# MLP in blocks of 1024 columns, two of eight k-tile groups by Strassen's seven products

## The chip, the cores and the metric

The kernel runs on one core of one Trainium2 chip. The metric is device time in microseconds of one execution; lower is better. The profile was taken of one such execution.

## What is computed

One decoder layer for 256 tokens with a model width of 2048, in fp32: three token mixers in parallel (gated convolution, attention with decay, attention to memory), merged by gates and projected, and then an MLP with a hidden width of 8192. Only the MLP is changed:

```python
h2 = _rms(x, norm2_g)
x = x + jnp.square(jax.nn.relu(h2 @ w_up)) @ w_down
```

`w_up` is 2048 x 8192 and `w_down` 8192 x 2048, each 64 MB in fp32.

## The kernel before, in words

Every large product runs in the same way. The stationary operand of TensorE is a 128 x 128 tile of activations (the tokens are two tiles of 128), the moving one is 512 columns of a weight row tile. To keep fp32 accuracy with the fp32r format each operand is split into a high part, its rounding, and a low part, the remainder, and each product is three matmuls: low x high, high x high, high x low (`products`, line 1083, matmuls at line 1096).

Weights come in pieces of 2 k tiles x 512 columns (512 KB) in a ring of four buffers, `raw`, `whi` and `wlo`. A piece passes through four engines: SyncE issues its load once the low part of the piece four earlier has been made (`load`, line 346, issue at line 353); ScalarE rounds it to `whi` once it has landed and TensorE has used the piece four earlier (`split`, lines 467 to 473); VectorE subtracts to get `wlo` (lines 718 to 721); TensorE does 2 k tiles x 2 token tiles x 3 = 12 matmuls on it. ScalarE and VectorE run through one fixed list of steps each, written out piece by piece; all other work is hung on piece numbers in that list.

A block is 8 pieces, 512 output columns for all 256 tokens, in two PSUM banks; blocks alternate between banks 0, 1 and 2, 3, so a block is emptied while the next one is computed. Banks 4 to 7 take transposes. The MLP has four quarters of the hidden width. In each, four up blocks give 2048 hidden columns: ScalarE applies the scale and relu from PSUM to `stage` (`relu`, line 663), VectorE squares (`square`, line 1004), TensorE transposes (line 1113, four 128 x 128 tiles to a bank), and ScalarE and VectorE write the high and low parts to `act_parts` (`plain_hi`, line 653, `plain_lo`, line 759). Four down blocks then multiply by `w_down` and VectorE adds the banks to `x_sb` (`add_to_x`, line 999). The first quarter is written out, the other three are a loop on every engine. At the end the last two bank tiles are added (line 1077) and stored in two transfers (line 438).

## Time and profile before

| | us |
|---|---|
| median of 3 runs | 1656.94 (1656.36 to 1657.6) |
| the profiled execution, its own time | 1656.12 |
| its span, first to last instruction | 1654.4 |
| TensorE busy, 7500 matmuls | 1646.7 |
| weight loads of TensorE busy | 1363.3 |
| VectorE busy | 911.1 |
| ScalarE busy | 750.1 |

PE is TensorE, PEld its weight loads, DVE VectorE, ACT ScalarE, SP SyncE, and SPq its queue of DMA issues. In a line of a timeline the first number is the start in us from the span's start, the second the time taken; "x2" means that two instructions were merged; brackets hold the idle time before it and what ended it. Matmuls are pipelined, so the durations of neighbours overlap.

### The profile page before, as it was taken

How to read it: one execution, taken by the hardware profiler on the slowest of the kernel's cores; microseconds unless marked ns; L12 is line 12 of the kernel's file. 1: busy time of each engine (PE TensorE's matmuls, PEld its weight loads, DVE VectorE, ACT ScalarE, POOL GpSimd, SP SyncE). 2: the span in 40 equal slices, each digit the busy share in tenths (PEclk: the TensorE clock that was granted, in tenths of full speed). 3: DMA queues.
4: the chain of work that ended last, by engine and by line, in shares of the span. 5: the costliest groups of instructions: out<-in, count | busy, mean ns of one | idle time of the engine just before them, and what ended most of it. 6: DMA issues, size and time to landing. Idle time of an engine off the chain costs nothing.

```text
span 1654.4 us, 19971 instructions
## 1 busy us (share of the span) xinstructions
PE 1646.7 (100%) x7500; PEld 1363.3 (82%) x7500; DVE 911.1 (55%) x1004; ACT 750.1 (45%) x878; POOL 4.8 (0%) x13
## 2 busy tenths in 40 slices
PE   9999999999999999999999999999999999999998
PEld 7888888888888888888888888888888888888887
DVE  5856666545565444456665555545555555555553
ACT  6744444443444444444445544434443444334432
POOL 0000000000000000000000000000000000000000
PEclk9999999999999999999999999999999999999999
DMA  9856555566566666665655666666566665666554
GB/s 336 280 167 187 166 168 164 154 179 176 166 184 186 192 195 194 191 193 182 197 186 185 186 185 179 198 192 189 181 191 193 191 187 184 195 192 184 184 189 152
DMA packets 160176, 313.49 MB, mean 189 GB/s; under 512 B 9584, under 2 KB 9968, under 8 KB 159600
## 3 DMA queue, kind: packets, MB, share of 16 engines
q1 hardware_dynamic: 160112, 312.62, 62.2%
q8 instruction: 42, 0.69, 0.2%
q14 instruction: 22, 0.18, 0.0%
HBM read 310.49 MB, written 2.10 MB: 189 GB/s over the span
## 4 chain that ended last, share of the span: by engine, by line
PE 98%; DMA 1%; DVE 0%; ACT 0%; SPq 0%; issue 0%; DVEq 0%; ACTq 0%
PE bank L1096 94%; PE bank L1113 2%; PE bank L1125 1%; DMA raw<-in_w_mem_kv 1%; PE bank L1220 0%; PE bank L1150 0%; PE bank L1181 0%; DVE wlo L721 0%; PE bank L1240 0%; ACT whi L473 0%; PE bank L1145 0%; PE bank L1242 0%; DVE wide L806 0%; SPq L362 0%; PE bank L1151 0%
## 5 line engine op out<-in xcount | busy, mean ns | idle before, releaser
L721 DVE TENSOR_TENSOR wlo<-raw,whi 128x1024 fp32r<-128x1024 f32 x574 | 701.5, 1224 | 673.1 <-ACT whi L473 670.2
L473 ACT ACTIVATE whi<-raw 128x1024 fp32r<-128x1024 f32 x574 | 608.2, 1060 | 778.5 <-PE bank L1096 764.6
L1096 PE MATMUL bank<-whi,lhs_a 128*128 128x512 f32 x1920 | 597.6, 392 | 0.0
L1096 PE MATMUL bank<-whi,lhs_b 128*128 128x512 f32 x1536 | 476.5, 391 | 2.0 <-DVE wlo L744 1.3
L1096 PEld LDWEIGHTS bank<-whi,lhs_a 128*128 128x128 f32 x1920 | 357.1, 188 | 71.8
L1096 PE MATMUL bank<-wlo,lhs_a 128*128 128x512 f32 x960 | 374.3, 390 | 0.0
L1096 PEld LDWEIGHTS bank<-whi,lhs_b 128*128 128x128 f32 x1536 | 285.9, 188 | 61.4 <-issue 3.5
L1096 PE MATMUL bank<-whi,act_parts 128*128 128x512 f32 x1024 | 316.1, 390 | 0.0
L1096 PE MATMUL bank<-wlo,lhs_b 128*128 128x512 f32 x768 | 299.3, 390 | 0.0
L1096 PEld LDWEIGHTS bank<-whi,act_parts 128*128 128x128 f32 x1024 | 191.7, 188 | 39.4
L1096 PEld LDWEIGHTS bank<-wlo,lhs_a 128*128 128x128 f32 x960 | 180.2, 188 | 38.3
L1096 PE MATMUL bank<-wlo,act_parts 128*128 128x512 f32 x512 | 199.3, 389 | 0.0
L1096 PEld LDWEIGHTS bank<-wlo,lhs_b 128*128 128x128 f32 x768 | 144.2, 188 | 30.5
L1096 PEld LDWEIGHTS bank<-wlo,act_parts 128*128 128x128 f32 x512 | 96.1, 188 | 20.1
L482 ACT ACTIVATE wide<-bank,sm 128x512 f32<-128x512 f32 (+1 forms) x48 | 30.4, 684 | 36.8 <-PE bank L1096 36.4
L1096 PE MATMUL bank<-whi,y_parts 128*128 128x512 f32 x128 | 40.1, 394 | 0.0
L1004 DVE TENSOR_TENSOR stage<-stage 128x1024 f32<-128x1024 f32 x16 | 19.6, 1225 | 27.3 <-ACT stage L663 27.3
L663 ACT ACTIVATE stage<-bank,sm 128x512 f32<-128x512 f32 x32 | 20.3, 685 | 26.6 <-PE bank L1096 26.6
L999 DVE TENSOR_TENSOR x_sb<-bank,x_sb 128x512 f32<-128x512 f32 x38 | 24.5, 686 | 8.3 <-PE bank L1096 8.3
L1096 PEld LDWEIGHTS bank<-whi,y_parts 128*128 128x128 f32 x128 | 23.6, 188 | 4.7
L1096 PE MATMUL bank<-wlo,y_parts 128*128 128x512 f32 x64 | 25.0, 391 | 0.0
L1113 PEld LDWEIGHTS bank<-ident,stage 128*128 128x128 f32 x160 | 19.8, 139 | 5.2
(133 smaller groups left out, 472.1 us busy)
## 6 DMA issues: line engine op xcount, KB each, us to landing
raw<-in_w_in SPq DMA_DIRECT2D x208, 512.0 KB, 3.7
raw<-in_w_up SPq DMA_DIRECT2D x128, 512.0 KB, 3.7
raw<-in_w_down SPq DMA_DIRECT2D x128, 512.0 KB, 3.8
raw<-in_w_out SPq DMA_DIRECT2D x32, 512.0 KB, 3.7
raw<-in_w_mem_kv SPq DMA_DIRECT2D x30, 512.0 KB, 6.3
raw<-in_w_conv_out SPq DMA_DIRECT2D x16, 512.0 KB, 3.8
raw<-in_w_fox_out SPq DMA_DIRECT2D x16, 512.0 KB, 3.9
raw<-in_w_mem_out SPq DMA_DIRECT2D x16, 512.0 KB, 4.5
```

What stands on the lines that cost most here:

```text
L473: act.activation(whi[n % RING][:], raw[n % RING][:], ACT.Copy).then_inc(hi_ready, 1)
L482: last = act.activation(outs[tok], src, func, scale=scale[:, tok:tok + 1])
L663: last = act.activation(stage[:, tok, :], bank[2 * (b % 2) + tok][:], ACT.Relu, scale=r_2[:, tok:tok + 1])
L721: dve.tensor_tensor(wlo[n % RING][:], raw[n % RING][:], whi[n % RING][:].bitcast(F32), ALU.subtract).then_inc(lo_ready, 1)
L999: last = dve.tensor_tensor(v, bank[2 * (b % 2) + tok][:], v, ALU.add)
L1004: dve.tensor_tensor(stage[:], stage[:], stage[:], ALU.mult).then_inc(sq_ready, 1)
L1096: last = pe.matmul(dst, lhs[:, part, k + kk, s], w[:, kk, :], start=(k + kk == 0 and i == 0), stop=(k + kk == tiles - 1 and i == 2))
L1113: last = pe.transpose(bank[tr_bank(g)][:, P * i:P * (i + 1)], src, ident[:])
L1125: last = pe.matmul(dst, a, b, start=(i == 0), stop=(i == len(pairs) - 1))
```

## The change

The MLP is computed in 16 blocks of 1024 columns, per quarter two up blocks and two down blocks of 8 groups; a group is 2 k tiles x 1024 columns, two pieces (left and right). In six groups each piece takes 12 matmuls as before, the left one into banks 0 and 1, the right one into banks 2 and 3. In groups 3 and 6 the product of the 2 x 2 tiles of activations (2 token tiles x 2 k tiles) with the 2 x 2 tiles of weights (2 k tiles x 2 halves of 512 columns) is done with Strassen's seven products (Winograd's form), each of three matmuls. Three of them add straight into the banks C12, C21 and C11, and P5, P6, P7 and P1 are summed over both groups in banks 4 to 7.

For this VectorE makes four sums of raw weight tiles, T (`t_sums`), which ScalarE rounds and VectorE subtracts (`sums_hi`, `sums_lo`); only tiles 1 to 3 of such a group are split themselves (`split_fast`, 1536 columns in one instruction for both pieces). Four sums of activation tiles, S, are made once per quarter and group (`a_copy`, `s_sums`, `s_hi`, `s_lo`). At the turn of a block ScalarE copies P1 and then banks 0, 1 and banks 2, 3 to SBUF (`c_copy`, into `stage` and `junk`), VectorE makes the corrections from P5, P6, P7 and the copy of P1 (`combine`), and adds them: for an up block to the copies, with relu and square both on ScalarE after it; for a down block x is first added to the corrections (`x_to_sums`) and later the copies (`result`). The transposes of the activations now use banks 4 to 7 ahead of group 3. `act_parts` shares its space with `lhs_a`, and the last block of `w_out` uses banks 4 and 5.

The core of the diff (the engine programs; the helpers for S, the operand parts and the loads' order are left out):

```diff
+FAST = (3, 6)
+GROUPS = KT // PK
+WIDE = 2 * COLS
+FF_BLOCKS = 2 * D // WIDE
+UPS = D // WIDE
+FF_PIECES = FF_BLOCKS * 2 * GROUPS
+C22, C12, C21, C11, P5, P6, P7, P1 = range(8)
+S_1, S_2, S_3, S_4 = range(4)
+T_3, T_1, T_2, T_4 = range(4)
+def ff_piece(q, blk=0, g=0):
...
+                def c_copy(blk, side):
+                    at = FF_BLOCKS * q + blk
+                    act.wait_ge(piece_used, by_n + (ff_piece(q, blk) - 1 + side))
+                    act.wait_ge(ff_done, by_8 + 2 * (at - 1))
+                    act.wait_ge(tr_made, by_8 + (G_FF + GROUPS * (q if blk else q - 1) + 4 * min((blk - 1) % FF_BLOCKS, UPS)))
+                    act.activation(halves[side], bank_all[:, 2 * side:2 * side + 2, :], ACT.Copy).then_inc(c_out, 1)
...
+                for blk in range(FF_BLOCKS):
+                    after = q > 0 or blk > 0
+                    after_up = 0 < blk <= UPS
+                    at = FF_BLOCKS * q + blk
+                    left(blk, 0)
+                    if after:
+                        act.wait_ge(piece_used, by_n + (ff_piece(q, blk) - 2))
+                        act.wait_ge(ff_done, by_8 + 2 * (at - 1))
+                        act.activation(comb[:, 3, :], bank[P1], ACT.Copy).then_inc(p1_copied, 1)
+                    right(blk, 0)
+                    if after:
+                        c_copy(blk, 0)
+                        c_copy(blk, 1)
+                    left(blk, 1)
+                    right(blk, 1)
+                    if after_up:
+                        relu_square(blk, 0)
+                    left(blk, 2)
+                    if after_up:
+                        relu_square(blk, 1)
+                    right(blk, 2)
+                    sums_hi(2 * at, base=by_8)
+                    if after_up:
+                        act_hi(blk, 0)
+                    fast(blk, 3)
+                    if after_up:
+                        act_hi(blk, 1)
+                    left(blk, 4)
+                    right(blk, 4)
+                    if q == 0 and blk == 0:
+                        s_hi(1, 1, s_up)
+                    if after_up:
+                        s_hi(2 * q + blk + 1, blk - 1, s_down, base=2 * i)
+                    left(blk, 5)
+                    right(blk, 5)
+                    sums_hi(2 * at + 1, base=by_8)
+                    fast(blk, 6)
+                    left(blk, 7)
+                    right(blk, 7)
...
+            def t_sums(n, i, base=0, base16=0):
+                for u in range(2):
+                    dve.wait_ge(landed[(n + u) % RING], base16 + 16 * ((n + u) // RING + 1))
+                r = n % RING
+                b = raw_all[:, r:r + 2, :].rearrange("p r (k n) -> p (r k) n", k=PK)
+                b22, b21 = b[:, 1, :], b[:, 3, :]
+                dve.tensor_tensor(t_raw[:, 0:2, :], b[:, 1:3, :], b[:, 0:1, :].to_broadcast([P, 2, COLS]),
+                                  ALU.subtract).then_inc(t_made, 1)
+                dve.wait_ge(t_made, base * 3 + (3 * i + 1))
+                dve.tensor_tensor(t_raw[:, T_2, :], t_raw[:, T_1, :], b22, ALU.add).then_inc(t_made, 1)
+                dve.wait_ge(t_made, base * 3 + (3 * i + 2))
+                dve.tensor_tensor(t_raw[:, T_4, :], b21, t_raw[:, T_2, :], ALU.subtract).then_inc(t_made, 1)
+            def sums_lo(i, base=0):
+                dve.wait_ge(t_hi_ready, base * 2 + 2 * (i + 1))
+                dve.tensor_tensor(t_lo[:], t_raw[:], t_hi[:].bitcast(F32), ALU.subtract).then_inc(t_lo_ready, 1)
+            def split_fast(n, base=0):
+                r = n % RING
+                dve.wait_ge(hi_ready, base + (n + 2))
+                src, hi, lo = [w[:, r:r + 2, :].rearrange("p r n -> p (r n)")[:, COLS:]
+                               for w in (raw_all, whi_all, wlo_all)]
+                dve.tensor_tensor(lo, src, hi.bitcast(F32), ALU.subtract).then_inc(lo_ready, 2)
+            def combine(at, base=0):
+                dve.wait_ge(p1_copied, base + (at + 1))
+                dve.tensor_tensor(comb[:, 4, :], bank[P6], comb[:, 3, :], ALU.add).then_inc(combined, 1)
+                dve.wait_ge(combined, base * 3 + (3 * at + 1))
+                dve.tensor_tensor(comb[:, 2, :], bank[P7], comb[:, 4, :], ALU.add).then_inc(combined, 1)
+                dve.wait_ge(combined, base * 3 + (3 * at + 2))
+                dve.tensor_tensor(comb[:, 0:2, :], comb[:, 2:5:2, :],
+                                  bank[P5].unsqueeze(1).to_broadcast([P, 2, COLS]),
+                                  ALU.subtract).then_inc(combined, 1)
...
+            def x_to_sums(at, c, base=0):
+                dve.wait_ge(combined, base * 3 + 3 * (at + 1))
+                for side in range(2):
+                    v = comb[:, 2 * side:2 * side + 2, :]
+                    last = dve.tensor_tensor(v, v, x_half(c, side), ALU.add)
+                last.then_inc(x_in, 1)
+            def result(at, side, dst, base=0):
+                dve.wait_ge(c_out, base * 2 + (2 * at + side + 1))
+                dve.tensor_tensor(dst, halves[side], comb[:, 2 * side:2 * side + 2, :],
+                                  ALU.add).then_inc(ff_done, 1)
...
+                for blk in range(FF_BLOCKS):
+                    after = q > 0 or blk > 0
+                    after_up = 0 < blk <= UPS
+                    after_down = after and not after_up
+                    at = FF_BLOCKS * q + blk
+                    c = (blk - 1) % FF_BLOCKS - UPS
+                    left(blk, 0)
+                    if after:
+                        combine(at - 1, base=by_b)
+                    right(blk, 0)
+                    if after_up:
+                        dve.wait_ge(combined, by_b * 3 + 3 * at)
+                        result(at - 1, 0, halves[0], base=by_b)
+                    left(blk, 1)
+                    if after_up:
+                        result(at - 1, 1, halves[1], base=by_b)
+                    if after_down:
+                        x_to_sums(at - 1, c, base=by_b)
+                    right(blk, 1)
+                    left(blk, 2)
+                    t_sums(ff_piece(q, blk, 3), 2 * at, base=by_8, base16=by16)
+                    right(blk, 2)
+                    sums_lo(2 * at, base=by_8)
+                    if after_up:
+                        act_lo(blk, 0)
+                    fast(blk, 3)
+                    if after_up:
+                        act_lo(blk, 1)
+                    left(blk, 4)
+                    if q == 0 and blk == 0:
+                        s_sums(1, 1)
+                    if after_up:
+                        s_sums(2 * q + blk + 1, blk - 1, base=2 * i)
+                    right(blk, 4)
+                    if after_down:
+                        dve.wait_ge(x_in, i * UPS + (UPS * (q if blk else q - 1) + c + 1))
+                        for side in range(2):
+                            result(at - 1, side, x_half(c, side), base=by_b)
+                    left(blk, 5)
+                    if q == 0 and blk == 0:
+                        s_lo(1, 1, s_up)
+                    if after_up:
+                        s_lo(2 * q + blk + 1, blk - 1, s_down, base=2 * i)
+                    t_sums(ff_piece(q, blk, 6), 2 * at + 1, base=by_8, base16=by16)
+                    right(blk, 5)
+                    sums_lo(2 * at + 1, base=by_8)
+                    fast(blk, 6)
+                    left(blk, 7)
+                    right(blk, 7)
...
+            def half_group(n, side, g, lhs):
+                pe.wait_ge(lo_ready, n + 1)
+                hi, lo = whi[n % RING], wlo[n % RING]
+                for kk in range(PK):
+                    for tok in range(TOK):
+                        for i, (part, w) in enumerate(((1, hi), (0, hi), (0, lo))):
+                            last = pe.matmul(bank[2 * side + tok],
+                                             lhs[:, part, PK * g + kk, P * tok:P * (tok + 1)], w[:, kk, :],
+                                             start=(g + kk == 0 and i == 0),
+                                             stop=(g == GROUPS - 1 and kk == PK - 1 and i == 2))
+                last.then_inc(piece_used, 1)
+            def fast_group(n, g, lhs, sums):
+                u, r = FAST.index(g), n % RING
+                b22, b11, b21 = [[w[:, r:r + 2, :].rearrange("p r (k n) -> p (r k) n", k=PK)[:, c, :]
+                                  for w in (whi_all, wlo_all)] for c in (1, 2, 3)]
+                t1, t2, t3, t4 = [(t_hi[:, c, :], t_lo[:, c, :]) for c in (T_1, T_2, T_3, T_4)]
+                a11, a12 = [[lhs[:, part, PK * g + c, P:2 * P] for part in range(2)] for c in range(PK)]
+                a22 = [lhs[:, part, PK * g + 1, 0:P] for part in range(2)]
+                s1, s2, s3, s4 = [[sums[:, part, u, c, :] for part in range(2)]
+                                  for c in (S_1, S_2, S_3, S_4)]
+                def product(at, a, b):
+                    own = at >= P5
+                    for i, (part, w_part) in enumerate(((1, 0), (0, 0), (0, 1))):
+                        ins = pe.matmul(bank[at], a[part], b[w_part], start=(own and u == 0 and i == 0),
+                                        stop=(own and u == len(FAST) - 1 and i == 2))
+                    return ins
+                product(P5, s1, t1)
+                product(P6, s2, t2)
+                product(P7, s3, t3)
+                product(C21, a22, t4).then_inc(t_used, 1)
+                pe.wait_ge(lo_ready, n + 2)
+                product(C12, s4, b22)
+                product(P1, a11, b11)
+                product(C11, a12, b21).then_inc(piece_used, 2)
+            def act_transposes(q, blk, side):
+                pe.wait_ge(sq_ready, 2 * (UPS * q + blk - 1) + side + 1)
+                for a in range(2):
+                    transposes(G_FF + GROUPS * q + 4 * (blk - 1) + 2 * side + a,
+                               token_tiles(halves[side], PK * a), bk=4 + 2 * side + a)
+            for q in range(QUARTERS):
+                for blk in range(FF_BLOCKS):
+                    at = FF_BLOCKS * q + blk
+                    lhs, sums = (lhs_b, s_up) if blk < UPS else (act_parts, s_down)
+                    for g in range(GROUPS):
+                        n = ff_piece(q, blk, g)
+                        if g in FAST:
+                            if at == 0:
+                                wo_events(n)
+                                wo_events(n + 1)
+                                pe.wait_ge(tr_taken, G_X2 + g + 1)
+                                pe.wait_ge(s_lo_ready, FAST.index(g) + 1)
+                            if blk == UPS:
+                                pe.wait_ge(tr_taken, G_FF + GROUPS * q + g + 1)
+                                pe.wait_ge(s_lo_ready, 2 * (q + 1) + FAST.index(g) + 1)
+                            if g == FAST[0] and at == 0:
+                                pe.wait_ge(dve_emptied, emptied(B_FF - 1))
+                                pe.wait_ge(tr_taken, G_FF)
+                            elif g == FAST[0]:
+                                pe.wait_ge(combined, 3 * at)
+                                if 0 < blk <= UPS:
+                                    pe.wait_ge(tr_taken, G_FF + GROUPS * q + 4 * blk)
+                            pe.wait_ge(t_lo_ready, 2 * at + FAST.index(g) + 1)
+                            fast_group(n, g, lhs, sums)
+                            continue
+                        if g == 2 and 0 < blk <= UPS:
+                            act_transposes(q, blk, 1)
+                        for side in range(2):
+                            if g == 0 and at == 0:
+                                pe.wait_ge(dve_emptied, emptied(B_WO + 2))
+                            elif g == 0:
+                                pe.wait_ge(c_out, 2 * (at - 1) + side + 1)
+                            if at == 0:
+                                wo_events(n + side)
+                                pe.wait_ge(tr_taken, G_X2 + g + 1)
+                            if blk == UPS:
+                                pe.wait_ge(tr_taken, G_FF + GROUPS * q + g + 1)
+                            if g == 1 and side == 1 and 0 < blk <= UPS:
+                                act_transposes(q, blk, 0)
```

## Rows read from the trace of the kernel before

**Rows 1.** The page: engine totals, and the granted clock in 40 slices.
```profile
PE 1646.7 (100%) x7500; PEld 1363.3 (82%) x7500; DVE 911.1 (55%) x1004; ACT 750.1 (45%) x878; POOL 4.8 (0%) x13
...
PEclk9999999999999999999999999999999999999999
```

**Rows 2.** Busy time by stretch: us, PE, PEld, DVE, ACT, POOL, clock, DMA share, GB/s.
```profile
1310.00:1353.50 43.50, 43.50 (x202) 35.98 (x200) 23.41 (x22) 20.20 (x24) 0.00 (x0) 1.00 0.62 188
```

**Rows 3.** Timeline of one MLP piece: start us, us, engine, line, operation, idle before.
```profile
1302.16 0.39 PE L1096 MATMUL bank<-wlo,lhs_b 128*128 128x512 f32 x1
...
1302.59 1.06 ACT L473 ACTIVATE whi<-raw 128x1024 fp32r<-128x1024 f32 x1 [1.66 <-PE bank L1096]
...
1303.68 1.23 DVE L721 TENSOR_TENSOR wlo<-raw,whi 128x1024 fp32r<-128x1024 f32 x1 [1.50 <-ACT whi L473]
...
1305.31 1.06 ACT L473 ACTIVATE whi<-raw 128x1024 fp32r<-128x1024 f32 x1 [1.66 <-PE bank L1096]
```

**Rows 4.** Timeline of SyncE's queue: the load issued behind that piece's subtraction.
```profile
1305.07 0.37 SPq L353 DMA_DIRECT2D raw<-in_w_up  x1
```

**Rows 5.** Timeline of ScalarE (first three) and VectorE around two groups of transposes.
```profile
1321.63 1.06 ACT L473 ACTIVATE whi<-raw 128x1024 fp32r<-128x1024 f32 x1 [1.66 <-PE bank L1096]
1322.60 0.58 ACT L653 ACTIVATE act_parts<-bank 128x512 fp32r<-128x512 f32 x1
1324.85 1.06 ACT L473 ACTIVATE whi<-raw 128x1024 fp32r<-128x1024 f32 x1 [1.67 <-PE bank L1096]
...
1322.73 1.23 DVE L721 TENSOR_TENSOR wlo<-raw,whi 128x1024 fp32r<-128x1024 f32 x1 [1.49 <-ACT whi L473]
1323.87 0.68 DVE L759 TENSOR_TENSOR act_parts<-bank,act_parts 128x512 fp32r<-128x512 f32 x1
```

**Rows 6.** Groups of instructions: shapes, count, busy us, mean ns, idle before.
```profile
L721 DVE TENSOR_TENSOR wlo<-raw,whi 128x1024 fp32r<-128x1024 f32 x574 | 701.5, 1224 | 673.1 <-ACT whi L473 670.2
L473 ACT ACTIVATE whi<-raw 128x1024 fp32r<-128x1024 f32 x574 | 608.2, 1060 | 778.5 <-PE bank L1096 764.6
...
L759 DVE TENSOR_TENSOR act_parts<-bank,act_parts 128x512 fp32r<-128x512 f32 x32 | 21.8, 683 | 0.0
...
L653 ACT ACTIVATE act_parts<-bank 128x512 fp32r<-128x512 f32 x32 | 18.6, 581 | 0.0
```

**Rows 7.** Line 353's loads: landings, a pair issued (its second landed in 4.6), two in flight.
```profile
DMA to landing us min/median/max: 3.4/3.7/4.8
...
DMA to landing us min/median/max: 4.6/4.6/4.6
...
1342.73 1.75 SPq L353 DMA_DIRECT2D raw<-in_w_up  x2
...
1323.00:1324.00 1.00, 1.00 (x6) 0.79 (x5) 1.00 (x2) 0.18 (x1) 0.00 (x0) 1.00 0.98 346
```

**Rows 8.** Timeline of an early wait of TensorE, and the stretch 9 to 12 us.
```profile
13.08 1.23 DVE L721 TENSOR_TENSOR wlo<-raw,whi 128x1024 fp32r<-128x1024 f32 x1 [0.62 <-ACT whi L473]
...
13.30 0.39 PE L1096 MATMUL bank<-wlo,lhs_b 128*128 128x512 f32 x1
...
14.45 0.70 PE L1096 MATMUL bank<-whi,lhs_b 128*128 128x512 f32 x2 [0.76 <-DVE wlo L721]
...
14.99 0.40 PE L1096 MATMUL bank<-wlo,lhs_b 128*128 128x512 f32 x1
...
9.00:12.00 3.00, 2.25 (x11) 1.56 (x10) 2.12 (x5) 2.37 (x6) 0.00 (x0) 1.00 0.98 357
```

**Rows 9.** Timeline of the end, and the landing of the two last stores (line 438).
```profile
1649.84 0.39 PE L1096 MATMUL bank<-wlo,act_parts 128*128 128x512 f32 x1
1650.27 1.29 DVE L1077 TENSOR_TENSOR x_sb<-bank,x_sb 128x512 f32<-128x512 f32 x2 [8.56 <-PE bank L1096]
1650.99 0.94 SPq L438 DMA_DIRECT2D out<-x_sb  x2
...
DMA to landing us min/median/max: 2.4/2.4/2.4
```

390 lines of the change are left out of this document (236 added, 154 removed).

## The prediction

> **What bounds the kernel now.** I read the totals and the slices first [rows 1]: TensorE is busy for the whole span at full granted clock, VectorE for 55% and ScalarE for 45%. So only TensorE work removed, or a wait that TensorE is given, can move the time. One stretch of the MLP that holds 16 pieces shows the room beside it [rows 2]: in 43.5 us VectorE works 23.4 us. Then the timeline gives the rhythm [rows 3]. ScalarE's `whi` copy starts at 1302.59 and again at 1305.31, each released by TensorE: 2.72 us per piece of 12 matmuls, 0.2267 us a matmul. A piece's last matmul starts at 1302.16 and ends at 1302.55, 0.16 us behind its slot; ScalarE starts 0.04 us later, VectorE 0.03 us after ScalarE. The load of a free `raw` buffer is issued 0.16 us after VectorE's subtraction ended at 1304.91 [rows 4]. Engines start the next of two ready instructions about 0.09 us before the first ends [rows 5]: VectorE 1.14 us after a 1024-wide start, ScalarE 0.97 us. Today piece n is split as soon as piece n-4 is used, so it is ready some 5.8 us early (three pieces, 8.16 us, less 2.35 us of split).
>
> **The saving.** Per block of 1024 columns a fast group issues 7 products of 3 matmuls, 21, where the two pieces issued 24. There are 16 blocks with two fast groups: 32 x 3 = 96 matmuls fewer, at 0.2267 us: **-21.8 us**. The diff counts them, so "it does not save them" is no rival. All are 512 wide and on 128 x 128 weights as before, and banks already alternate every three matmuls. The trace's pitch is 227 ns. The Trainium skill, TensorE: Matmul & The Clock Gate, "Wait - 56ns, not 53.3ns?", gives 512/2.4 + 2.5 = 215.8 ns for a warm matmul; by that the saving would be 20.7 us. The trace's number stands.
>
> **What is added, by engine.** All of it is on ScalarE and VectorE. From the groups [rows 6] I take VectorE 1.22 us for 1024 elements and 0.68 for 512, hence 1.77 for 1536 and 2.31 for 2048; ScalarE 1.06 for 1024 from SBUF and, between 0.58 (one bank) and 1.16 (two such), 1.0 for two banks. A block then asks of VectorE 12 subtractions (13.7 us), 2 wider ones (3.3), 2 T sums (5.3), 2 T subtractions (4.4), the combination (2.6), two results (2.3), and either x added to the sums (2.3) or operand parts and S sums (3.8): 34 to 36 us in a block that lasts 40.4 us without transposes. It fits on average; it does not fit in order, since VectorE runs strictly in order and two pieces of cover are all that four buffers give when the T sums must see both raw pieces of a group.
>
> **Blocks that follow an up block (8 of 16).** Count from the end of the last matmul of the block before. ScalarE copies banks 2, 3 (from 0.04), splits piece 2 (0.95 to 2.01). VectorE: lo of piece 2 at 2.05, the second half's result 3.19, lo of piece 3 4.33 to 5.55. That frees the buffer of piece 7: load issued 5.71, landed 9.4 with 3.7 us [rows 7]. The T sums wait for exactly this: 1.22 + 0.68 + 0.68 and two hand-overs, 12.1. ScalarE rounds the second half of T, 13.2. VectorE: T subtraction (next start 15.4), two operand parts (16.6), the 1536 split (18.3), two operand parts, done 19.6. TensorE may not start group 3 before, because the transposes of those parts sit in banks 4 to 7 where P5, P6, P7 and P1 go, and the last two parts come behind the wide split in VectorE's order. TensorE itself gets there after six pieces and four transposes of about 0.48 us (3.22 against 2.72 in [rows 5]): 16.3 + 1.9 - 0.16 = 18.1. A late release costs more than its lateness: the early wait [rows 8] is released at 14.31, the matmul starts at 14.45, and the first two take 0.54 us instead of 0.45, so 0.23 us in all. Stall: 19.6 + 0.23 - 18.1 = 1.75, **8 x 1.8 = +14.4 us**.
>
> **Blocks that follow a down block (7 of 16).** Same start; after lo of piece 2, x is added to the sums (2 x 1.14), lo of piece 3 ends at 6.7, the load lands 10.6, the T sums leave VectorE at 13.15, and only then comes lo of the right piece of group 2, at 14.4. That small subtraction is queued behind a wait for a transfer. TensorE has had five pieces: 13.6 - 0.16 = 13.4. Stall 14.4 + 0.23 - 13.4 = 1.2, **7 x 1.2 = +8.1 us**. Behind the fast group four loads are released nearly together (18.5, 19.0, 19.6, 20.8). At the 346 GB/s of two loads in flight [rows 7] 512 KB take 1.5 us, so the fourth lands at 26.8, its T sums and the lo of group 5's right piece end at 30.6, and TensorE would be there at 30.2 (2.72 + 21 matmuls + 3 pieces after 14.6): 0.5 us, **+3.7 us**. In blocks after an up block TensorE is later by then, and I charge nothing; if that cover went it would be this same 0.5 us, eight times.
>
> **Costed at nothing.** The first block of the MLP has no combination, and its last x2 operand parts come behind the wide split with about 2 us in hand. Bank turnover without a second pair of banks: banks 0, 1 are copied during the last right piece, banks 2, 3 within 1.0 us of its end while TensorE has a left piece of 2.72 us. P1, P6, P7, P5 are read over 4 us, two pieces before group 3 wants them. Loads are as many and as large.
>
> **The tail.** Now 1.3 us of additions after the last matmul, then two 256 KB stores that land 2.4 us after issue [rows 9]. After: group 6 ends 5.4 us before the last slot; copy of P1, combination (2.6), x to the sums (2.3), a 1024-wide addition, two of 512: the last ends 2.9 us after the last slot against 1.5, and a 512 KB store goes just ahead of the two small ones, 0.4 us more. Between +1.4 and +2.3 (the store queue at read speed or slower); I take **+1.8 us**.
>
> **Sum.** -21.8 + 14.4 + 8.1 + 3.7 + 1.8 = +6.2 us. Against the profiled execution's 1656.12 us that is 1662.3; it lay 0.8 us under the median of the runs, so **1663 us**.
>
> **Bounds.** The chains repeat 22 times with no cushion, so a tenth of a microsecond in each is 2.2 us. Landing was 3.4 to 4.8 us [rows 7]: at 3.4 the sum falls by 6.6; at 4.0, about halfway to the late row of 4.6, it rises by 6.6. Bunched loads at 1.3 or 1.8 us each move it by -3 or +5. One-sided jitter only adds.
>
> **Rivals.**
> 1. Loads come sooner than the T sums ask (3.4 us, and a shorter queue), so the down blocks lose both stalls: -21.8 + 14.4 + 1.8 = -5.6, 1651 us; if VectorE's order also keeps up in the up blocks, 1637. It ends faster, and it decides from where all stalls together are under 16.7 us. For it: VectorE has some 5 us free per block. Against: the chain holds 3.7 us of landing in series with 10 us of ordered work.
> 2. Bunched loads are dearer than single ones. One issued 1.38 us behind another landed in 4.6 us [rows 7]. If pairs cost that 0.9 us more, group 6 stalls 15 times by another 0.5 to 0.9: +8 to +14 more, about 1673 us.
> 3. The waits lower the clock. The early stretch with 2.25 of 3 us busy kept the granted clock at 1.00 [rows 8], and none here is longer than 2 us. If nevertheless the 12 matmuls behind each of 22 waits ran at 1.2 GHz, twice the pitch, that is +60 us, 1723. The Trainium skill, TensorE: Matmul & The Clock Gate, "A second HAM failure mode: psum-queue depth-cycling", says that short idles between groups of matmuls, with banks cycled each iteration, make the clock swing; it speaks against this change, and the early rows do not show it.
>
> **How the numbers follow.** Forecast 0.55, by itself 1657 to 1669; rival 1 0.20, rival 2 0.20, rival 3 0.05. Against the median 1656.94, 0.2% is 3.3 us, about what a measurement of this kernel can tell. Slower: 0.42 of the forecast's 0.55, 0.20 and 0.05: 0.67. Faster: 0.16 of rival 1. Same: the rest, 0.17. The range leaves out rival 3, the far part of rival 1 and the end of rival 2: 1650 to 1673.
>
> **What would show it.** Right: TensorE matmuls 96 fewer; idle of TensorE of some 26 us, about 1.6 to 1.8 at group 3 of up-following blocks, released by VectorE's operand part, and about 1.2 at the right piece of group 2 elsewhere, released by `wlo`; VectorE busy near 1090 us, waiting for `raw` loads ahead of the T sums. Wrong: TensorE idle under 17 us in the MLP, waits on the bank copies or the squared activations instead, or a granted clock under 1.00 inside the span.

## The result: slower, by five times what was forecast

| kernel | median us | runs |
|---|---|---|
| before | 1656.67 | 4 (1656.36 to 1657.6) |
| changed | 1688.17 | 4 (1681.17 to 1689.01) |

The ratio is 1.018, 95% interval 1.0152 to 1.0207: +31.5 us where +6 was forecast, outside the range of 1650 to 1673. One execution of the kernel before, in a later round of runs, took 4315.09 us at a granted clock of 1.00; it is left out of every comparison, and why it took so long is not known. The profiled execution took 1689.01 us, its span is 1687.3 us, 32.9 us longer than before.

The page of the changed kernel, engine totals and granted clock:

```profile
PE 1642.3 (97%) x7404; PEld 1354.5 (80%) x7404; DVE 1104.8 (65%) x1199; ACT 851.2 (50%) x1002; POOL 4.8 (0%) x13
...
PEclk9999999999999999999999999999999999999999
```

Against [rows 1], TensorE has 96 matmuls fewer, 7404 for 7500, as counted in the diff. VectorE went from 911 to 1105 us (about 1090 was forecast). The line of the granted clock shows nothing in 40 slices, but its mean over the span is 0.991, where it was 1.000.

The chain of releases shows where TensorE stood. These lines give the waiting engine, tile and line, what it waited for, the total in us, the number of times and the longest:

```profile
DVE t_raw L1187 <- DMA raw<-in_w_down: 35.4, 12, 3.4
...
DVE t_raw L1187 <- DMA raw<-in_w_up: 26.9, 11, 3.7
...
PE bank L1601 <- DVE wlo L882: 14.7, 14, 1.7
...
PE bank L1621 <- DVE lhs_a L920: 11.1, 4, 3.1
...
PE bank L1621 <- issue: 8.4, 4, 3.3
```

TensorE waits 22 times in the MLP, and in no other places than the forecast named: eight times at group 3 of a block behind an up block (line 1621; "issue" and `lhs_a` are the same wait, for the operand parts), and fourteen times at a right piece (line 1601), seven at group 2 and seven at group 5. Ahead of that, VectorE waits for `raw` in front of its T sums. The sizes were not as forecast:

| term | forecast | measured |
|---|---|---|
| 96 matmuls at 0.2267 us | -21.8 | -21.8 |
| group 3, 8 waits | +14.4 | 19.4 idle + 8 x 0.25 = +21.4 |
| right piece of group 2, 7 waits | +8.1 | 7.7 + 7 x 0.25 = +9.4 |
| right piece of group 5, 7 waits | +3.7 | 7.0 + 7 x 0.25 = +8.8 |
| clock | 0 | +12.0 |
| tail | +1.8 | +2.4 |
| sum | +6.2 | +32.2, of 32.9 in the span |

The 0.25 us added to each idle time of the timeline is what the idle time does not count: the last matmul's end lies 0.16 us behind its slot, and the first pair behind a wait is 0.09 us longer [rows 3, 8].

**The chain, block by block.** VectorE's timeline behind an up block, whose last matmul ended at 1027.17 (start us, us, engine, line, operation; x2 are two merged, brackets the idle time before):

```profile
1029.20 1.23 DVE L882 TENSOR_TENSOR wlo<-raw,whi 128x1024 fp32r<-128x1024 f32 x1 [0.22 <-ACT whi L527]
1030.35 1.22 DVE L1230 TENSOR_TENSOR junk<-junk,comb 128x1024 f32<-128x1024 f32 x1
1031.48 1.22 DVE L882 TENSOR_TENSOR wlo<-raw,whi 128x1024 fp32r<-128x1024 f32 x1
...
1037.76 1.23 DVE L1187 TENSOR_TENSOR t_raw<-raw 128x1024 f32<-128x1024 f32 x1 [3.12 <-DMA raw<-in_w_down]
1039.02 0.69 DVE L1190 TENSOR_TENSOR t_raw<-t_raw,raw 128x512 f32<-128x512 f32 x1
1039.75 0.69 DVE L1192 TENSOR_TENSOR t_raw<-raw,t_raw 128x512 f32<-128x512 f32 x1
1040.36 1.22 DVE L882 TENSOR_TENSOR wlo<-raw,whi 128x1024 fp32r<-128x1024 f32 x1
1041.57 2.29 DVE L1196 TENSOR_TENSOR t_lo<-t_raw,t_hi 128x2048 fp32r<-128x2048 f32 x1
1043.78 1.28 DVE L920 TENSOR_TENSOR lhs_a<-bank,lhs_a 128x512 fp32r<-128x512 f32 x2
1044.98 1.75 DVE L1203 TENSOR_TENSOR wlo<-raw,whi 128x1536 fp32r<-128x1536 f32 x1
1046.64 1.28 DVE L920 TENSOR_TENSOR lhs_a<-bank,lhs_a 128x512 fp32r<-128x512 f32 x2
```

The schedule of the prediction put the subtraction of piece 3 from 4.33 to 5.55 us after the block's end; it ran from 4.31 to 5.53. From the first T sum to the end of the last operand part it had 10.2 us; the trace has 1037.76 to 1047.92, 10.16. What it had wrong stands between: the load behind that subtraction, in SyncE's timeline with its landing.

```profile
1032.73 0.37 SPq L407 DMA_DIRECT2D raw<-in_w_down  x1
...
DMA to landing us min/median/max: 4.9/4.9/4.9
```

It landed 4.9 us after issue, not 3.7. The T sums start at 10.6 instead of 9.4, and everything behind them keeps that 1.2 us. The other blocks agree: in the eight blocks behind an up block this load landed 3.7 to 5.3 us after issue, 4.4 on average, and the idle time at group 3 was 1.8 to 2.2 us less than the landing in each of them. In the seven behind a down block it landed in 3.8 to 4.2 us, 3.9 on average.

**The clock.** TensorE's timeline at the wait this leads to:

```profile
1044.90 0.39 PE L1601 MATMUL bank<-wlo,lhs_a 128*128 128x512 f32 x1
...
1048.18 1.19 PE L1621 MATMUL bank<-t_hi,s_down 128*128 128x512 f32 x2 [2.89 <-DVE lhs_a L920]
1049.17 0.63 PE L1621 MATMUL bank<-t_lo,s_down 128*128 128x512 f32 x1
...
1054.90 0.39 PE L1621 MATMUL bank<-wlo,lhs_a 128*128 128x512 f32 x1
1055.13 0.63 PE L1621 MATMUL bank<-whi,lhs_a 128*128 128x512 f32 x2
```

After a wait of 2.89 us two matmuls take 1.19 us instead of 0.70. Stretches by engine (span, PE, PEld, DVE, ACT and POOL busy, granted clock, DMA share, GB/s):

```profile
1040.00:1048.00 8.00, 5.29 (x24) 4.04 (x22) 8.00 (x9) 6.96 (x11) 0.00 (x0) 0.95 0.21 68
1048.00:1054.00 6.00, 5.82 (x14) 4.60 (x15) 3.09 (x6) 0.63 (x1) 0.00 (x0) 0.50 0.91 302
```

The granted clock is 0.50 there, the lower of its two levels, 1.2 instead of 2.4 GHz, and the pitch is 0.427 us instead of 0.227. The execution has six such stretches in the MLP, 27.3 us in all, 25.0 of them with TensorE at work. In and beside them 61 matmuls start later than their 0.2267 us behind the one before, by 12.0 us together. Each lies at one of the group-3 waits: at all five with more than 2.5 us of idle and at one of 1.82 us; the two others, of 1.47 and 1.76 us, have none behind them.

A long wait does not bring it every time. In all the traces of this case every half-rate stretch of the MLP (the tail after the last matmul left out) lies at a wait of 1.8 us or more, but some long waits have none: 2.98 us in the kernel with the right pieces ahead of the T sums, 2.35 us in the one with half loads, 2.18 us in the changed kernel's second trace, and 3.23 us in the kernel with more work on VectorE, this stretch (the kernels are described below):

```profile
1180.00:1200.00 20.00, 16.77 (x74) 13.58 (x73) 16.82 (x21) 12.18 (x16) 0.00 (x0) 1.00 0.50 157
```

What tells the one kind from the other is open. The Trainium skill, TensorE: Matmul & The Clock Gate, "A second HAM failure mode: psum-queue depth-cycling", describes frequent short idles between groups of matmuls that make the clock swing. The fourteen waits of 0.3 to 1.7 us at right pieces come nearest to that, and the clock stayed at 1.00 behind them; it fell at the long ones only.

**The tail.** The last matmul, the last additions and the last stores:

```profile
1680.31 0.39 PE L1601 MATMUL bank<-wlo,lhs_a 128*128 128x512 f32 x1
...
1682.17 1.28 DVE L1370 TENSOR_TENSOR x_sb<-bank,comb 128x512 f32<-128x512 f32 x2
1682.88 1.16 SPq L492 DMA_DIRECT2D out<-x_sb  x2
```

The last matmul's slot ends at 1680.54 and the additions end at 1683.45, 2.9 us later as reckoned (1.5 in [rows 9]). The span ends 6.8 us after the slot against 4.3, since the two last stores also land later, 3.3 us after issue where it was 2.4.

### The profile page after: what moved, and what is told of

The parts are those of the page before. It is cut to its first block, busy times and chain, and to the rows that moved or that the text cites. A ratio compares the mean times of both kernels' runs of the same rounds, so it can differ in the third digit from the quotient of the medians.

```text
span 1687.3 us, 20278 instructions
## 1 busy us (share of the span) xinstructions
PE 1642.3 (97%) x7404; PEld 1354.5 (80%) x7404; DVE 1104.8 (65%) x1199; ACT 851.2 (50%) x1002; POOL 4.8 (0%) x13
## 4 chain that ended last, share of the span: by engine, by line
PE 79%; DVE 8%; DMA 7%; issue 4%; ACT 1%; SPq 0%; DVEq 0%; ACTq 0%
PE bank L1389 51%; PE bank L1601 17%; PE bank L1621 8%; DMA raw<-in_w_down 4%; DVE wlo L882 3%; DMA raw<-in_w_up 2%; PE bank L1406 1%; DVE t_raw L1187 1%; ACT whi L527 1%; PE bank L1419 1%; DVE comb L1224 1%; DVE t_raw L1190 1%; DMA raw<-in_w_mem_kv 1%; DVE lhs_a L920 0%; DVE wlo L1203 0%
## 5 line engine op out<-in xcount | busy, mean ns | idle before, releaser
L882 DVE TENSOR_TENSOR wlo<-raw,whi 128x1024 fp32r<-128x1024 f32 x510 | 622.0, 1224 | 486.5 <-ACT whi L527 483.4
L527 ACT ACTIVATE whi<-raw 128x1024 fp32r<-128x1024 f32 x510 | 535.6, 1059 | 577.5 <-PE bank L1389 393.6
L1389 PE MATMUL bank<-whi,lhs_a 128*128 128x512 f32 x1920 | 598.2, 393 | 0.0
L1389 PEld LDWEIGHTS bank<-whi,lhs_a 128*128 128x128 f32 x1920 | 357.3, 188 | 71.7
L1389 PE MATMUL bank<-wlo,lhs_a 128*128 128x512 f32 x960 | 374.8, 390 | 0.0
L1601 PE MATMUL bank<-whi,lhs_a 128*128 128x512 f32 x768 | 238.5, 392 | 9.8 <-DVE wlo L882 9.8
L1601 PE MATMUL bank<-whi,lhs_b 128*128 128x512 f32 x768 | 238.5, 392 | 4.9 <-DVE wlo L882 4.9
L1389 PEld LDWEIGHTS bank<-wlo,lhs_a 128*128 128x128 f32 x960 | 180.3, 188 | 38.0
L1601 PEld LDWEIGHTS bank<-whi,lhs_a 128*128 128x128 f32 x768 | 143.1, 188 | 42.1 <-DVE wlo L882 13.2
L1389 PE MATMUL bank<-whi,lhs_b 128*128 128x512 f32 x512 | 158.3, 391 | 2.7 <-DVE wlo L882 1.7
L1601 PE MATMUL bank<-wlo,lhs_a 128*128 128x512 f32 x384 | 149.8, 390 | 0.0
L730 ACT ACTIVATE t_hi<-t_raw 128x1024 fp32r<-128x1024 f32 x64 | 67.9, 1061 | 110.6 <-DVE t_raw L1187 98.9
L1389 PEld LDWEIGHTS bank<-whi,lhs_b 128*128 128x128 f32 x512 | 95.8, 188 | 23.1 <-issue 3.5
L1601 PEld LDWEIGHTS bank<-wlo,lhs_a 128*128 128x128 f32 x384 | 72.1, 188 | 15.1
L1187 DVE TENSOR_TENSOR t_raw<-raw 128x1024 f32<-128x1024 f32 x32 | 39.1, 1223 | 62.3 <-DMA raw<-in_w_down 35.4
L1196 DVE TENSOR_TENSOR t_lo<-t_raw,t_hi 128x2048 fp32r<-128x2048 f32 x32 | 73.4, 2293 | 0.0
L1203 DVE TENSOR_TENSOR wlo<-raw,whi 128x1536 fp32r<-128x1536 f32 x32 | 56.0, 1751 | 0.0
```

Of the source, the lines that this page charges most:

```text
L527: act.activation(whi[n % RING], raw[n % RING], ACT.Copy).then_inc(hi_ready, 1)
L730: act.activation(t_hi[:, 2 * h:2 * h + 2, :], t_raw[:, 2 * h:2 * h + 2, :], ACT.Copy).then_inc(t_hi_ready, 1)
L882: dve.tensor_tensor(wlo[n % RING], raw[n % RING], whi[n % RING].bitcast(F32), ALU.subtract).then_inc(lo_ready, 1)
L1187: dve.tensor_tensor(t_raw[:, 0:2, :], b[:, 1:3, :], b[:, 0:1, :].to_broadcast([P, 2, COLS]), ALU.subtract).then_inc(t_made, 1)
L1196: dve.tensor_tensor(t_lo[:], t_raw[:], t_hi[:].bitcast(F32), ALU.subtract).then_inc(t_lo_ready, 1)
L1203: dve.tensor_tensor(lo, src, hi.bitcast(F32), ALU.subtract).then_inc(lo_ready, 2)
```

## The experiments

Each is the changed kernel with one edit, unless it says otherwise. Times are medians; a run of the kernel before beside each gave 1656.6 to 1657.4 us.

### Is VectorE's total work the bound? (1682.4 us)

```diff
+                    if after:
...
+                        for dst in (prob[:, 0:512], prob_t[:, 0:512]):
+                            v = ident[:].unsqueeze(1).to_broadcast([P, 4, P])
+                            dve.tensor_tensor(dst.rearrange("p (a n) -> p a n", a=4), v, v,
+                                              ALU.add).then_inc(idle_done, 1)
                     t_sums(ff_piece(q, blk, 3), 2 * at, base=by_8, base16=by16)
```

> VectorE gets two more 512-wide additions in each of 15 blocks, 1.2 us, where it now idles about 3 us for the raw pieces of group 3 (their results are used by nothing). Theory (landing in series, VectorE waits there anyway): no change within 3 us, 1685 to 1691 us, and VectorE's idle ahead of the first T sum falls by 1.2 us a block. Rival (VectorE's total work sets the time): +1.2 us x 15 = +18 us, about 1706 us.

18 us of work were added (VectorE was busy 1123.6 us for 1104.8) and the time did not rise. The waits of the T sums took it up:

```profile
DVE t_raw L1188 <- DMA raw<-in_w_down: 24.3, 12, 3.4
DVE t_raw L1188 <- DMA raw<-in_w_up: 18.3, 12, 3.2
```

They fell from 62.3 us in all to 42.6. VectorE is not short of time; what it does in this gap is free. The changed kernel alone varied from 1681 to 1689 us in its six runs, with a median of 1686.6, so 1682.4 (two runs) is not shown to be a gain either.

### The same kernel again (1684.5 us), and the kernel before again (1656.8 us)

> The changed kernel once more, unaltered: the 22 waits at the same places, their sizes 0.3 to 3.3 us and the number of half-rate stretches varying with where the loads land. 1681 to 1689 us. If the waits at group 3 come out under 2 us, fewer half-rate stretches and a time near 1681.

> The kernel before, once more with a trace, to see how long loads take to land in the stages that the change leaves alone. If the later landing there in the changed kernel (4.1 us median for w_out against 3.7) is a matter of the execution, this trace shows 3.7 to 4.7 at random; if it is a matter of the program, it shows 3.7 again. 1656 to 1658 us either way.

The changed kernel has the same 22 waits, 31.1 us of idle for 34.1, and four half-rate stretches in the MLP instead of six, which cost 7.5 us instead of 12.0. Landings are medians in us after the name, operation, count and KB; first the changed kernel of the result, then the kernel before in its second trace:

```profile
raw<-in_w_up SPq DMA_DIRECT2D x128, 512.0 KB, 4.0
raw<-in_w_down SPq DMA_DIRECT2D x128, 512.0 KB, 4.4
```

```profile
raw<-in_w_up SPq DMA_DIRECT2D x128, 512.0 KB, 3.7
raw<-in_w_down SPq DMA_DIRECT2D x128, 512.0 KB, 4.4
```

In its first trace the kernel before had 3.7 and 3.8. So the landing of `w_down` is no constant of the kernel: one execution had 3.8, another 4.4, and nothing of it showed in a time of 1656.8 us, since every load was then covered by some 4 us. The expectation "again 3.7, or at random" came out as the second. Why `w_down` lands later than `w_up` was not tried.

Even the first trace, from which the prediction was read, holds a stretch in which nothing but the late value occurs. This is the line for the eight loads issued from 1256 to 1277.5 us, all of `w_down`, 2.72 us apart or more:

```profile
DMA to landing us min/median/max: 4.6/4.7/4.8
```

In the changed kernel the blocks whose loads are of `w_down` carry it for the most part: at group 3 of the second up-following block of each quarter, the first down block, the wait was 2.5 to 3.1 us in the first trace and 2.2 to 2.7 in the second. In the first up-following block of the first quarter, fed by `w_up`, it was 1.47 us, or 1.7 with its 0.25: the forecast's 1.75. But the same block of the second quarter, fed by `w_up` as well, had the longest wait of each trace, 3.31 and 3.38 us, because this one load landed in 5.25 and 5.57 us. So the tensor alone does not settle it.

### Does the clock fall because of the waits? (1677.1 us)

```diff
                                 if 0 < blk <= UPS:
+                                    for _ in range(12):
+                                        pe.matmul(bank[0], prob[:, 0:64].bitcast(BF16),
+                                                  prob[:, 0:256].bitcast(BF16), start=False, stop=False)
                                     pe.wait_ge(tr_taken, G_FF + GROUPS * q + 4 * blk)
```

> TensorE runs 12 extra matmuls of zeros, 512 columns, 2.7 us, into the wait at group 3 of the eight blocks that follow an up block (they add zero to bank 0), and VectorE clears their operand once. Theory (waits of over about 2 us lower the clock to half for what follows): granted clock 1.00 throughout the MLP, the extra matmuls cost 0 to 1 us each time where the wait was shorter, the half-rate stretches (27 us, some 13 us lost) go: 1676 to 1684 us. Rival (the half-rate stretches are chance and unconnected with the waits): clock stays near 0.991 and the time rises to 1688 to 1696 us.

TensorE's timeline at the same wait, and the stretch behind it:

```profile
1045.83 2.54 PE L1666 MATMUL bank<-prob 128*128 128x512 bf16 x11
1048.56 0.74 PE L1623 MATMUL bank<-t_hi,s_down 128*128 128x512 f32 x2 [0.19 <-DVE lhs_a L921]
...
1048.00:1056.00 8.00, 7.81 (x35) 6.13 (x34) 4.83 (x9) 2.64 (x3) 0.00 (x0) 1.00 0.79 255
```

The filler (2.7 us of matmuls whose result is zero) leaves 0.19 us of idle, the granted clock is 1.00 where it was 0.50, and there is no half-rate stretch in the MLP. The kernel is 11 us faster than the changed one for 96 more matmuls, or 9.5 us against the median of the changed kernel's six runs. So the clock falls because TensorE stands still at these waits, and the term of 12.0 us has the right size. The gain is not its exact price: where the wait was shorter than 2.7 us the filler takes time of its own, and there are only two runs, 1675.7 and 1678.4 us.

### The landing by itself (1650.0 us)

```diff
+            def half_load(n, src, base=None):
+                sp.wait_ge(lo_ready, (0 if base is None else base) + (n - RING + 1))
+                sp.dma_start(raw[n % RING][:, 0:1, :], src).then_inc(landed[n % RING], 16)
...
-                k = slice(PK * g, PK * (g + 1))
+                k = slice(PK * g, PK * g + 1)
...
-                    load(n, src, base=i * FF_PIECES)
+                    half_load(n, src, base=i * FF_PIECES)
```

> Each load of the MLP brings only the first k tile of its piece, 256 KB instead of 512 KB, and leaves the second as it was: the MLP is computed with stale weights there. All instructions of TensorE, ScalarE and VectorE stay. Theory (landing is in series in every one of the 22 waits): landing falls from about 4.2 to 2.5-3.0 us, all waits shrink by 1.2 to 1.7 us: group 2 and 5 waits go, group 3 waits fall to 0.3-1.0, no half-rate stretch: 1640 to 1650 us. Rival (VectorE's and ScalarE's own work): waits at group 3 stay over 1.5 us, above 1670 us.

Landing fell to 2.8 (`w_up`) and 3.2 us (`w_down`). As expected, the fourteen waits at right pieces are gone (three of 0.1 us are left). The eight at group 3 are left with somewhat more than expected, 0.45 to 1.3 us and one of 2.35, and no half-rate stretch is left in the MLP. The time fell by 38 us with every instruction of the compute engines in place. By the ledger that is all of the 18 us at right pieces, 11 of the 21 at group 3, and the 12 of the clock: 41 us, of which 38 were measured. The changed kernel's own runs vary by more than the difference. Half loads land earlier singly and in bunches, so the run shows what the landings cost in all and does not split it.

### Orders, and a later wait

**Operand parts ahead of the wide split (1678.1 us).** In the lists of ScalarE and VectorE:

```diff
                     if after_up:
                         act_lo(blk, 0)
-                    fast(blk, 3)
-                    if after_up:
                         act_lo(blk, 1)
+                    fast(blk, 3)
```

> ScalarE and VectorE make the last two operand parts of a block ahead of the wide split of group 3 instead of behind it; nothing else moves. Theory (a chain from the landing of the last raw piece of group 3 through the T sums and the operand parts ends the wait at group 3, and waits of over about 2 us cost clock as well): the eight waits at group 3 shrink by 1.7 us each, from 1.5-3.3 us of idle to 0-1.6; the half-rate stretches after them go; waits at the right pieces of groups 2 and 5 stay. About 1688 - 13 - 13 = 1660 to 1666 us. Rival (VectorE is short of time as a whole, so the wait only moves to the next thing in its order): TensorE waits as long in group 3 for the split pieces, 1685 to 1690 us.

A miss by 12 us (three runs, 1671.0 to 1679.8). The waits at group 3 shrank as reckoned (0.3 to 1.7 us; two are gone), but the wide split now ends 1.2 us later, with it the loads of group 5 that it releases, and TensorE gets to group 5 earlier: the right piece there, which had no wait in up-following blocks, now waits in all eight of them, 0.3 to 3.6 us and 1.0 on average. The prediction had priced that cover at 0.5 us. Two half-rate stretches are left, at waits of 3.6 and 1.9 us.

**Piece 3 ahead of the second result (1663.4 us).**

```diff
                     left(blk, 1)
+                    right(blk, 1)
                     if after_up:
                         result(at - 1, 1, halves[1], base=by_b)
                     if after_down:
                         x_to_sums(at - 1, c, base=by_b)
-                    right(blk, 1)
```

> VectorE subtracts the right piece of group 1 ahead of the second half's result (after up blocks) or of adding x to the sums (after down blocks), so that the load of the last piece of group 3 is issued 1.14 or 2.27 us earlier. Theory (the landing is in series): the waits at group 3 shrink by about 1 us and those at the right piece of group 2 by 1.1 to 1.3, to near nothing; half-rate stretches go where the wait comes under 2 us; 1688 - 8 - 8 - about 10 = 1660 to 1670 us. If loads closer together land later by as much, the gain is under half of that. Rival (VectorE's total work): no change, 1685 to 1690 us.

As expected: one line moved gives 25 us (six runs, 1661.6 to 1670.2). Sixteen waits and 18.7 us of idle are left, and one half-rate stretch in the MLP, at a wait of 2.15 us.

**Right pieces ahead of the T sums (1697.8 us).**

```diff
-                    t_sums(ff_piece(q, blk, 3), 2 * at, base=by_8, base16=by16)
                     right(blk, 2)
+                    t_sums(ff_piece(q, blk, 3), 2 * at, base=by_8, base16=by16)
```

and likewise at group 5.

> Only: VectorE subtracts the right pieces of groups 2 and 5 ahead of the T sums instead of behind them. Theory: the wait at those right pieces goes, but the T sums wait for the same landing, so a wait of 0.5 to 1 us stands at groups 3 and 6 in its place; the waits after up blocks are as before. 1688 - 3 to - 10 = 1678 to 1685 us. Rival (the small subtraction's place in the queue was the cause): the 14 waits go without a successor, -18 us, 1670 us.

Wrong in sign: 10 us slower. VectorE's timeline in the same block of the changed kernel (second trace), then of this one:

```profile
989.98 1.23 DVE L882 TENSOR_TENSOR wlo<-raw,whi 128x1024 fp32r<-128x1024 f32 x1 [0.72 <-ACT whi L527]
993.09 1.22 DVE L1187 TENSOR_TENSOR t_raw<-raw 128x1024 f32<-128x1024 f32 x1 [1.88 <-DMA raw<-in_w_up]
...
995.68 1.22 DVE L882 TENSOR_TENSOR wlo<-raw,whi 128x1024 fp32r<-128x1024 f32 x1
```

```profile
990.15 1.23 DVE L882 TENSOR_TENSOR wlo<-raw,whi 128x1024 fp32r<-128x1024 f32 x1 [0.71 <-ACT whi L527]
993.41 1.23 DVE L882 TENSOR_TENSOR wlo<-raw,whi 128x1024 fp32r<-128x1024 f32 x1 [2.04 <-ACT whi L527]
994.55 1.22 DVE L1187 TENSOR_TENSOR t_raw<-raw 128x1024 f32<-128x1024 f32 x1
```

The right piece of group 2 is now what VectorE waits for. ScalarE rounds it only behind the two relus and the square of the second half, so the T sums, whose pieces had landed, start at 994.55 instead of 993.09, and the wait at group 3 went from 1.5 to 2.8 us. In blocks behind a down block the wait moved from the right piece to the group that follows it, as expected, at about the same size. What the expectation had wrong is that "the waits after up blocks are as before": at group 3 they came to 24.2 us where there were 19.4, and the execution has eight half-rate stretches in the MLP.

**All three (1666.5 us).**

> All three changes of order at once: the last operand parts ahead of the wide split, the right piece of group 1 ahead of the second result or of adding x, and the right pieces of groups 2 and 5 ahead of the T sums. Theory (chain from the landing): the down blocks' waits at right pieces go, waits at group 3 fall under 1 us, the waits left are those of group 6 behind four bunched loads, some 0.5 to 1 us in about 15 blocks; no half-rate stretches. 1637 with no wait at all, 1640 to 1655 us expected. Rival (VectorE's total work, or the bank turnover): 1655 to 1665 us, no better than the one order alone.

A miss by 11 us, and no better than the one good order alone. 20 waits and 21.8 us of idle are left: eight of the waits are at group 3 behind an up block, 1.1 to 2.0 us, and most of the others are at the low parts of the T sums. That these are the faults of the other two orders is likely from their own traces and not shown apart.

**The late wait (1675.3 us).** P5 and P6 need banks 4 and 5 alone; the last two operand parts sit in banks 6 and 7:

```diff
-                product(P7, s3, t3)
-                product(C21, a22, t4).then_inc(t_used, 1)
+                product(C21, a22, t4)
+                if parts is not None:
+                    pe.wait_ge(tr_taken, parts)
+                product(P7, s3, t3).then_inc(t_used, 1)
...
-                                    pe.wait_ge(tr_taken, G_FF + GROUPS * q + 4 * blk)
+                                    pe.wait_ge(tr_taken, G_FF + GROUPS * q + 4 * blk - 2)
```

> TensorE starts group 3 of the eight blocks after an up block once the operand parts in banks 4 and 5 are taken (P5 and P6 go there), runs C21, and waits for those in banks 6 and 7 only ahead of P7, nine matmuls (2.0 us) later. Nothing changes on ScalarE and VectorE. Theory: the last two parts, behind the wide split, end the wait; waits at group 3 fall from 1.5-3.4 us to 0-0.9 and the half-rate stretches go, while the right piece of group 5, now reached earlier, gets 0.5 to 1.1 us in those eight blocks: 1686 - 17 - 12 + 6 = 1660 to 1666 us. Rival (the T sums' low parts end the wait as well, they come out 2 us later than reckoned): no change at group 3, 1682 to 1688 us.

A miss by 9 us. At group 3 2.5 us of idle are left of 19.4, so the last parts did end that wait. Right pieces, above all of group 5, paid it back again, 23.1 us of idle in 21 waits where there were 14.7 in 14, up to 2.3 us at one piece; one of the three runs took 1666.4 us, the others 1675.3 and 1676.5.

### The version that beats both (1654.7 us)

The late wait, piece 3 ahead of the second result, and on ScalarE the left piece of group 1 rounded in the idle time ahead of the copy of banks 2 and 3:

```diff
                         c_copy(blk, 0)
-                        c_copy(blk, 1)
                     left(blk, 1)
+                    if after:
+                        c_copy(blk, 1)
                     right(blk, 1)
```

> The late wait, with the loads of group 3's last piece made earlier: ScalarE rounds the left piece of group 1 while it would idle ahead of the copy of banks 2 and 3, and VectorE subtracts the right piece of group 1 ahead of the second result or of adding x. Theory: the chain from the landing fits into the five or six pieces of cover in every block; left are waits of about 0.6 us at the right piece of group 5 in 15 blocks and the longer tail: 1656.7 - 21.8 + 9 + 2 = 1646 us, 1642 to 1652, faster than before. Rival (landing grows as loads come closer together, as at the bunched ones): waits of about 1 us stay at groups 5 and 6, 1652 to 1660 us.

Ratio to before 0.9984, interval 0.9973 to 0.9995 (10 runs, 1650.0 to 1657.2): it beats the kernel before, by 0.16%, barely. It took 2.7 us more than the slower end of what was expected. The profiled execution took 1650.9 us, one of the three fastest. In it twelve waits with 9.2 us of idle are left, 7.7 of them at group 5 in blocks fed by `w_down`. VectorE at one of them, and the landings of the two loads issued between 1222 and 1226:

```profile
1226.32 0.68 DVE L1178 TENSOR_TENSOR s_down<-s_raw,s_down 128x512 fp32r<-128x512 f32 x1
1229.93 1.23 DVE L1188 TENSOR_TENSOR t_raw<-raw 128x1024 f32<-128x1024 f32 x1 [2.93 <-DMA raw<-in_w_down]
...
DMA to landing us min/median/max: 6.0/6.0/6.0
...
DMA to landing us min/median/max: 5.6/5.6/5.6
```

Two loads behind a fast group took 6.0 and 5.6 us to land. The load on the chain at group 3, now issued 1.13 to 1.86 us behind the one before, landed in 4.8 us on average in up-following blocks and 5.1 in down-following ones, where it had been 4.4 and 3.9. Both sides of the expectation were half right: the chain of group 3 fits, and bunched loads still do not.

### With half loads as well (1636.7 us)

The same kernel with loads of the first k tile alone; half of the MLP's weights are stale.

> The late wait and the earlier loads together with loads of 256 KB in the MLP (only the first k tile of each piece is brought; the rest of its weights is stale). All work of TensorE, ScalarE and VectorE stays. Theory (22 waits in series with a landing, plus the clock that the long ones cost, are all that stood between the saving and the result): no wait of TensorE in the MLP over 0.3 us, clock 1.00, and the time is the one before less 96 matmuls at 0.2267 us plus a tail 1 to 2 us longer: 1656.7 - 21.8 + 1.5 = 1636.5 us, 1634 to 1640. Rival (something else of the change costs too, such as a slower pitch of the products or the bank turnover): 1642 us or more with no wait to show for it.

```profile
1000.00:1600.00 600.00, 600.00 (x2705) 497.93 (x2704) 486.50 (x455) 358.29 (x386) 0.00 (x0) 1.00 0.31 98
...
raw<-in_w_up SPq DMA_DIRECT2D x128, 256.0 KB, 2.8
raw<-in_w_down SPq DMA_DIRECT2D x128, 256.0 KB, 3.2
```

As expected, TensorE is busy 600.00 of 600 us at full clock, with no wait in the MLP, and the time is 1636.7 us (1636.1 to 1637.4). The saving of 21.8 us is real, products and bank turnover cost nothing of their own, and the tail takes some 2 us back.

## Why the prediction was wrong

The sign was right, and so were the places: all 22 waits, their releasers, the restart cost, the tail's additions, and "costed at nothing" for the bank turnover and the first block. The time is 26.0 us over the sum of +6.2: the ledger has 13.4 us of it in the waits, 12.0 in the clock and 0.6 in the tail. So two steps failed, and the prediction's own sign of being wrong, "a granted clock under 1.00 inside the span", is what the trace shows.

**The landing of 3.7 us.** The step said "load issued 5.71, landed 9.4 with 3.7 us". That was the median of a stretch in which one load was issued each 2.72 us and mostly from `w_up`. In the changed kernel medians were 4.0 and 4.4, and the load on the chain of group 3 landed in 4.4 us on average behind an up block and 3.9 behind a down block. The bounds had seen it coming in part ("at 4.0 it rises by 6.6"), yet stopped at 4.0, with a row of 4.6 in hand. These single landings account for most of 8.3 us: group 3 cost 21.4 for 14.4, and the right piece of group 2 9.4 for 8.1. The bunched loads are a size of their own: the fourth was to land 6.0 us after issue (released at 20.8, landed at 26.8) and took 5.6 to 7.2, 6.5 on average, and group 5 cost 8.8 us for 3.7. The half microsecond seven times is 3.5 of these 5.1 us; where the other 1.6 arise was not traced. Together that is the 13.4 us: 39.6 of waits against 26.2. Rival 2, dearer bunched loads, was therefore partly true, and the cover of group 5 in up-following blocks, priced at 0.5 us, cost 0.3 to 3.6 when two experiments took it away.

**"None here is longer than 2 us".** Rival 3 had 0.05 on it and hung on that sentence, which rested on the 3.7 us as well. Where the load landed in 4.4 to 5.3 us, the waits at group 3 came to 2.5 to 3.3 us, and the clock fell there. It was neither free nor the 60 us of the rival's price: 12.0 us, because it fell at six waits and not at 22. The two were not independent, as the chances had them: one error in the landing moved both.

One figure of the working is wrong without touching the sum: a block has 186 matmuls, 42.2 us at 0.2267 and not 40.4, so VectorE had some 7 us free per block and not 5.

What stays open is why `w_down` lands later, by a different amount from one stretch and one execution to the next, and why some waits of over 2 us left the clock alone.

## What to carry to other kernels

A schedule worked out from the rows of a profile held to 0.1 us for the instructions of VectorE compared above, and failed on the transfer and on the clock that a longer wait costs. Take a landing's late values, not its median, as soon as a wait is to be in series with it, since in a kernel that hides its loads the profile of before does not pay for them. When a change turns cover into waits, price the longest of them for the clock too, since a wait of 2.9 us there cost another 3. And before giving up such a change, look at which small instruction is queued behind which wait: one line moved was worth 25 of the 31 us.

## What the runs showed of the hardware

- The granted clock fell to 0.50 at waits of TensorE of 2.5 to 3.6 us, and at some of 1.82 to 2.4 us; in the MLP it stayed at 1.00 at every wait of up to 1.81 us, and also at some of 1.85 to 2.35 us and at those of 2.98 and 3.23 us. Matmuls of zeros in the wait kept it at 1.00. At 0.50 the pitch of 512-column matmuls was 0.427 us for 0.227.
- Landing of 512 KB in the changed kernel, medians for `w_up` and `w_down`: 3.8 and 4.0 us for loads issued over 4 us behind the one before, 4.2 and 4.8 at 1.7 to 2.5 us, 5.3 and 6.2 at under 1 us, 7.9 at most; of 256 KB 2.8 and 3.2 us over all. The Trainium skill, DMA: Bandwidth & Descriptors, "Latency and other measured facts", gives an HBM access 0.2 us on average and 2 us at high load. In the kernel before, loads 2.5 to 3 us apart landed in 3.4 to 5.7 us over its two traces, a spread of about that size, and no run here shows that it is the memory.
